# First panel of a two-block kernel by feature tiles, with squares on two engines, parameter rows issued around a square, and the 32-column panel in buffers of its own

## What is computed

```python
def _rms_norm(z, g):
    zf = z.astype(jnp.float32)
    zf = zf * lax.rsqrt(jnp.mean(zf * zf, axis=-1, keepdims=True) + RMS_EPS)
    return (zf * g.astype(jnp.float32)).astype(z.dtype)

def _token_mixer(xn, w_in, conv_a_w, shift_mu, w0, w2, a0, a2, g2, k_k, k_a, r_k, lnx_w, lnx_b, w_out):
    p = jnp.einsum('btd,de->bte', xn, w_in)
    gB, gC, hA = jnp.split(p[..., :3 * CONV_DIM], 3, axis=-1)
    ...
    q = p[..., 3 * CONV_DIM:]
    q = q + (_token_shift(q) - q) * shift_mu
    r, k, v, wd, ad, gd = jnp.split(q, splits, axis=-1)
    w_log = -jax.nn.softplus(-(w0 + jnp.tanh(wd) @ w2)) - 0.5
    decay = jnp.exp(-jnp.exp(w_log))
    a = jax.nn.sigmoid(a0 + ad @ a2)
    g = jax.nn.sigmoid(gd) @ g2
    kk = k4 * k_k;  kk = kk / jnp.maximum(jnp.linalg.norm(kk, axis=-1, keepdims=True), 1e-12)
    k4 = k4 * (1.0 + (a4 - 1.0) * k_a)
    ...
```

## Time and profile before

| | |
|---|---|
| median of 3 runs | 1960.25 us (1959.65 to 1961.53) |
| the profiled execution | 1962.35 us |
| its span in the trace | 1960.6 us |
| mean granted TensorE clock | 0.994 |
| PE busy | 1902.2 us, 12689 matmuls |
| DVE busy | 1154.5 us |
| ACT busy | 753.6 us |
| HBM read | 157.59 MB |

### The profile page before, as it was taken

How to read it: one execution, slowest core, us unless ns; L and a number is a source line. 1 busy time by engine, 2 the same in 40 slices (tenths; PEclk the granted TensorE clock), 3 DMA queues, 4 the chain that set the end, 5 groups by cost and what they waited for, 6 DMA issues and landing times.

```text
span 1960.6 us, 30342 instructions
## 1 busy us (share of the span) xinstructions
PE 1902.2 (97%) x12689; PEld 1536.9 (78%) x12689; DVE 1154.5 (59%) x1704; ACT 753.6 (38%) x1084; POOL 33.4 (2%) x72
## 2 busy tenths in 40 slices
PE   6989998999999999999999999999999999999999
PEld 4766777988888888787777778888778777778887
DVE  3574455677676336446687855455446678775544
ACT  4533423422222335533444334333533345334422
POOL 3000000020000000000000000000000000000000
PEclk9989999999999999999999999999999999999999
DMA  4221101433333232222222212233222212222232
GB/s 146 79 63 33 46 25 45 151 85 87 108 87 107 86 115 89 65 86 86 65 65 86 87 64 87 76 101 104 86 82 69 91 61 85 82 90 66 65 108 86
DMA packets 166036, 161.65 MB, mean 82 GB/s; under 512 B 13892, under 2 KB 150378, under 8 KB 165898
## 3 DMA queue, kind: packets, MB, share of 16 engines
q1 hardware_dynamic: 165200, 159.00, 25.9%
q10 hardware_dynamic: 698, 0.71, 0.1%
HBM read 157.59 MB, written 2.10 MB: 81 GB/s over the span
## 4 chain that ended last, share of the span: by engine, by line
PE 76%; DVE 2%; ACT 1%; issue 0%; ACTq 0%; DVEq 0%
PE psum L593 62%; PE psum L1911 5%; PE psum L2406 2%; PE psum L2383 1%; PE psum L583 1%; PE psum L2363 1%; PE psum L2391 1%; DVE w_lo L390 1%; PE psum L520 1%; ACT w_hi L349 1%; PE psum L529 0%; PE psum L2487 0%; DVE h_lo L454 0%; DVE ffn_normed L467 0%; PE psum L2472 0%; DVE w_lo L371 0%
## 5 line engine op out<-in xcount | busy, mean ns | idle before, releaser
L593 PE MATMUL psum<-h_hi,w_hi 128*128 128x512 f32 (+1 forms) x1592 | 622.4, 391 | 13.2 <-DVE h_lo L454 6.1
L593 PE MATMUL psum<-h_hi,w_lo 128*128 128x512 f32 (+1 forms) x1592 | 606.3, 381 | 0.0
L593 PE MATMUL psum<-h_lo,w_hi 128*128 128x512 f32 (+1 forms) x1592 | 606.2, 381 | 0.0
L390 DVE TENSOR_TENSOR w_lo<-w_raw,w_hi 128x2048 fp32r<-128x2048 f32 (+2 forms) x146 | 304.4, 2085 | 283.2 <-ACT w_hi L349 280.5
L349 ACT ACTIVATE w_hi<-w_raw 128x2048 fp32r<-128x2048 f32 (+1 forms) x151 | 265.0, 1755 | 370.9 <-PE psum L593 299.9
L593 PEld LDWEIGHTS psum<-h_hi,w_hi 128*128 128x128 f32 x1592 | 299.8, 188 | 92.8 <-issue 16.3
L593 PEld LDWEIGHTS psum<-h_hi,w_lo 128*128 128x128 f32 x1592 | 299.7, 188 | 58.4
L593 PEld LDWEIGHTS psum<-h_lo,w_hi 128*128 128x128 f32 x1592 | 300.1, 188 | 54.0 <-issue 0.2
L593 PE MATMUL psum<-w_hi,h_hi 128*128 128x512 f32 (+1 forms) x512 | 183.0, 357 | 2.7 <-DVE w_lo L390 1.8
L593 PE MATMUL psum<-w_lo,h_hi 128*128 128x512 f32 (+1 forms) x512 | 179.0, 350 | 0.0
L593 PE MATMUL psum<-w_hi,h_lo 128*128 128x512 f32 (+1 forms) x512 | 178.9, 349 | 0.0
(11 more groups left out here) (350 smaller groups left out, 2140.8 us busy)
## 6 DMA issues: line engine op xcount, KB each, us to landing
w_raw<-in_w_in_dram SPq DMA_DIRECT2D x170, 512.0 KB, 4.3
w_raw<-in_w_up_dram SPq DMA_DIRECT2D x44, 512.0 KB, 5.0
w_raw<-in_w_out_dram SPq DMA_DIRECT2D x24, 512.0 KB, 4.5
w_raw<-in_w_br_dram SPq DMA_DIRECT2D x48, 256.0 KB, 3.0
w_raw<-in_w_down_dram SPq DMA_DIRECT2D x22, 512.0 KB, 4.4
x_first<-in_x_dram SPq DMA_DIRECT2D x4, 512.0 KB, 4.9
x_tokens<-in_x_dram SPq DMA_DIRECT2D x4, 512.0 KB, 5.3
out_dram<-x_tokens SPq DMA_DIRECT2D x4, 512.0 KB, 2.6
```

Of the source, the lines that this page charges most:

```text
L390: eng.eng.tensor_tensor(m.wl[:, g % 2, 0:n], m.raw[:, g % 2, 0:n], m.wh[:, g % 2, 0:n].bitcast(F32), ALU.subtract).then_inc(eng.done, 1)
L593: last = pe.eng.matmul(out, a(k), b(k), start=(opens and k == 0 and i == 0), stop=(k == kt - 1 and i == 2), skip_group_check=ks is not None)
```

## The change

Buffers. Panel 0 now takes buffer 1 (`FIRST`), and the 32-column panel 1 has three small buffers of its own (`w1`, `w1H`, `w1L`, in the place of a decay tile that is written later). So panel 2 (buffer 0) is loaded and rounded without a wait, and panel 3 waits for panel 0.

ACT. A Sqrt of one constant stands first, and loads its table; POOL writes that constant before anything else. Six row loads, the square of x tile 0, the other six row loads, then the root of tiles 0 and 1 once DVE has squared tile 1 (a `tensor_tensor_reduce`), squares of tiles 2 and 3, their root, half of `w hi` 0, the eight `hH`, `w1 hi`, the row sums.

DVE. The square of tile 1; for each pair of tiles the reciprocal and the scaling, in halves of 512 columns (first halves of both tiles first), with the copy `params` between the pairs; the second half of `w hi` 0; the eight `hL` with the first half of `w lo` 0 behind the fourth and the second behind the eighth; `w1 lo`; the two `omm` steps.

PE. The sums table is turned without a wait for the rows. Feature tiles 0 to 3 are turned token tile by token tile, with the turn of the rows before token tile 2. Then for each feature tile k: two matmuls Whi·Hhi, two Whi·Hlo, and for k < 4 the turn of feature tile k + 4. Behind them panel 1's 16 with w1H, panel 0's 16 with wl, panel 1's 8 with w1L.

Later. PE runs half of panel 3 between the second and the third pair of `zw`, `za`. ACT and DVE split panel 2 in halves before shifted 0, panel 3 before shifted 2, panel 4 between the second and third pair (ACT) or behind k_scale 0 and 1 (DVE), and these two now stand before shifted 3 instead of behind decay_sum 1.

```diff
@@ lay_out
+    m.w1 = place("w_32_raw", [P, KT, 32], F32, m.Ep_at)
+    m.w1H = place("w_32_hi", [P, KT, 32], F32R, m.Ep_at + 4 * KT * 32)
+    m.w1L = place("w_32_lo", [P, KT, 32], F32R, m.Ep_at + 8 * KT * 32)
@@ constants
+    step(q.memset(m.eps[:, 0:1], RMS_EPS), "table 1")
+    step(q.memset(m.eps[:, 1:2], 1.0), "eps")
     step(q.memset(m.prow[:, :], 0.0), "prow zero")
...
@@ sync
+            if p == 1:
+                sp.dma_start(m.w1[:, :, :], s[:, :, c:c + w]).then_inc(w1_loaded, 16)
+                E.moved("w1 raw", "w1_loaded", 1)
+                continue
+            if p >= 3:
+                E.wait_ge(*E.point(("w lo", FIRST if p == 3 else p - 2)))
@@ tensor
-        turned("turn params", "params", [m.prow[:, :]])
-        turned("turn ind", ("ind", 1), [m.ind[:, i, :] for i in range(4)])
+        turn(E, m, banks, "turn ind", 3, ("ind", 1), [m.ind[:, i, :] for i in range(4)])
...
+        for t in range(TT):
+            if t == TT - 2:
+                E.wait_ge(*E.point("rows loaded"))
+                turn(E, m, banks, "turn params", 2, "params", [m.prow[:, :]])
+            E.wait_ge(*E.point(("n1", "xn a", t)))
+            for j in range(4):
+                last = pe.transpose(PS[:, 4 + j, P * t:P * t + P], m.xn1[:, t, P * j:P * j + P], m.ident[:, :])
...
+        E.wait_ge(act_done, E.at(("w hi half", FIRST)))
+        for k in range(KT):
+            E.wait_ge(act_done, E.at(("n1", "hi", k)))
+            if k == 4:
+                E.wait_ge(dve_done, E.at(("w hi", FIRST)))
+            for i in range(2):
+                pe.matmul(PS[:, i, :], H0[:, k, c0[i]], m.hH[:, k, :], start=k == 0, stop=False, skip_group_check=True)
+            E.wait_ge(dve_done, E.at(("n1", "lo", k)))
+            for i in range(2):
+                pe.matmul(PS[:, i, :], H0[:, k, c0[i]], m.hL[:, k, :], start=False, stop=False, skip_group_check=True)
+            if k < 4:
+                turn(E, m, banks, ("n1", "turn", k + 4), 4 + k, ("n1", "lo", k + 4),
+                     [m.xn1[:, t, P * (k + 4):P * (k + 4) + P] for t in range(TT)])
...
@@ tensor, zw and za
+            if j == 1:
+                panel(3, only=0)
-        panel(3)
+        panel(3, only=1)
@@ scalar
+        act.activation(m.stat[:, 5, 0:1], m.eps[:, 0:1], ACT.Sqrt).then_inc(act_done, 1)
...
+        rows_in(rowsrc[:6])
...
+        square(0)
+        rows_in(rowsrc[6:])
+        E.moved("rows loaded", "params_loaded", len(rowsrc))
+        E.wait_ge(dve_done, E.at(("n1", "ss", 1)))
+        root(0)
+        square(2)
+        square(3)
+        root(1)
...
@@ vector
+        dve.tensor_tensor_reduce(m.xn1[:, 1, :], m.x1[:, 1, :], m.x1[:, 1, :], 1.0, 0.0, ALU.mult, ALU.add,
+                                 m.stat[:, 0, 1:2]).then_inc(dve_done, 1)
...
+            for step, c in (("xn a", slice(0, D // 2)), ("xn", slice(D // 2, D))):
+                for t in (2 * g, 2 * g + 1):
+                    scaled(t, step, c)
+            if g == 0:
+                E.wait_ge(pe_done, E.at("turn params"))
+                dve.tensor_copy(m.pcol[:, :], PS[:, m.bank[E.key("turn params")], 0:P]).then_inc(dve_done, 1)
...
+        split(3)
+        shifted(2, then=False)
         E.wait_ge(act_done, E.at(("wsig", 0)))
         decay_sum(0)
+        k_scale(0)
+        k_scale(1)
+        split(4)
         shifted(3)
         E.wait_ge(act_done, E.at(("wsig", 1)))
         decay_sum(1)
-        k_scale(0)
-        k_scale(1)
```

More of the change, by code:

```diff
@@ new lines, in tensor @@
+        E.wait_ge(act_done, E.at("w1 hi"))
+        for k in range(KT):
+            for x in (m.hH, m.hL):
+                pe.matmul(PS[0:32, 2, :], H1[:, k, :], x[:, k, :], start=k == 0 and x is m.hH, stop=False,
+                          skip_group_check=True)
+        E.wait_ge(dve_done, E.at(("w lo", FIRST)))
+        for i in range(2):
+            for k in range(KT):
+                last = pe.matmul(PS[:, i, :], L0[:, k, c0[i]], m.hH[:, k, :], start=False, stop=k == KT - 1,
+                                 skip_group_check=True)
+            last.then_inc(pe_done, 1)
+            E.counted(("panel", 0, i))
@@ L736, in tensor @@
+        E.alias(("w used", FIRST), ("panel", 0, 1))
+        E.wait_ge(dve_done, E.at("w1 lo"))
+        for k in range(KT):
+            last = pe.matmul(PS[0:32, 2, :], L1[:, k, :], m.hH[:, k, :], start=False, stop=k == KT - 1,
+                             skip_group_check=True)
+        last.then_inc(pe_done, 1)
+        E.counted(("panel", 1, 0))
         E.wait_ge(*E.point("frows loaded"))
@@ L1103, in scalar, with rows_in, square @@
         E.wait_ge(act_done, E.so_far())
+        E.wait_ge(pool_done, E.at("eps"))
+        act.activation(m.stat[:, 5, 0:1], m.eps[:, 0:1], ACT.Sqrt).then_inc(act_done, 1)
+        E.counted(("n1", "table"))
         E.wait_ge(pool_done, E.at("prow zero"))
[L1105 to L1111, removed]
+        def rows_in(some):
+            for r0, src in some:
+                n, w = src.shape
+                act.dma_start(m.prow[r0:r0 + n, 0:w], src).then_inc(params_loaded, 16)
+        rows_in(rowsrc[:6])
+        def square(t):
+            E.wait_ge(act_done, E.so_far())
             E.wait_ge(*E.point(("x first", t)))
@@ L1134, in scalar @@
         E.wait_ge(act_done, E.so_far())
[L1135 to L1141, removed]
-        E.wait_ge(dve_done, E.at(("n1", "xn", TT - 1)))
+        E.wait_ge(dve_done, E.at(("n1", "xn", 3)))
         act.dma_start(m.w2a2[0:64, :], A["w2"][0]).then_inc(lr_loaded, 16)
@@ L1152, in scalar, with shifted @@
         z = 0
-        def shifted(p):
+        def shifted(p, then=True):
             nonlocal z
@@ L1166, in shifted @@
                 z += 1
-            split(p + 2)
+            if then:
+                split(p + 2)
         def decays(j):
@@ L1175, in decays @@
             E.counted(("Em", j))
-        shifted(0)
-        shifted(1)
+        split_hi_halves(E, m, 2, KT * panels[2][2])
+        shifted(0, then=False)
+        shifted(1, then=False)
         E.wait_ge(act_done, E.so_far())
@@ L1509, in prep @@
             E.counted(("prep", j))
-        shifted(0)
-        shifted(1)
+        split_lo_halves(E, m, 2, KT * panels[2][2])
+        shifted(0, then=False)
+        shifted(1, then=False)
         for b, n in ((0, FROWS), (1, FROWS2)):
```

133 lines of the change are left out of this document (85 added, 48 removed).

## The result

The changed kernel takes 1947.86 us (median of 4 runs, 1944.24 to 1949.99), against 1960.89 us for the kernel before (median of 4 runs beside them): a ratio of 0.9932, interval 0.9914 to 0.9949. The gain is 13.0 us where 16.3 were forecast; the median lies in the stated range (1939.5 to 1950.0), but outside the narrower forecast of 1940.7 to 1946.3. The profiled execution is the quickest of the four: 1944.24 us, span 1942.5, 18.1 us under the profiled execution of before. So what its trace shows has to be held against other executions before a term of the sum is judged by it.

A forecast was written before the change was run, and what follows sets the result against it. With TensorE busy 97% of the span, only its waits and low clock could yield gains. Gains of 8.8 + 6.3 + 1.2 = 16.3 us took the median of 1960.25 to 1944.0 us, range 1939.5 to 1950.0.

The forecast's parts named there:

- Rival A: Start gives less: rows up to 4 us late or clock low longer; gain 10 to 14, about 1948 us; chance 0.22.
- B: ACT replaces the bank wait between ffn rows and sum of squares; gain 4 to 10, about 1953 us; chance 0.09.
- D: hL or w_lo paces the first panel, PE reaches 43 as before; 0 to 4 us gained; chance 0.04.
- C: Wait before the spread shrinks by 2.6 us, or no clock fall there; 1938 to 1940.5 us; chance 0.08.
- Part 1: Start to the end of panels 0 and 1: ends at 34.9 instead of 43.69, gain 8.8 us, bounds 4 to 11.
- The first panel matmul: In the start: rows on PE at 11.5, first panel matmul at 14.7 against 25.52 before.
- The low rate: In the first panels: 3.5 us of low clock from 14.7 on, 1.8 us lost, bounds 0.7 and 5.1.
- The pacing: In the first panel: PE's 1.32 us per feature tile against DVE's 0.78, so PE, not h_lo, sets the pace.
- Rows and norm: In the start: rows land 4.9 us after last issue, at 11.5; squares and roots hidden, second table load gone.
- Part 2: Ffn rows to sum of squares: 38.0 becomes 31.7 us without bank wait or low clock; gain 6.3, bounds 2 and 6.5.
- Part 3: Wait of 6.58 us before the spread: two k scales earlier, gain 1.2 us (0 to 2.6).
- Everything after 115 us unchanged in length: From the chunk loop on: nothing changes in length, so what is gained by 115 us stays to the end.

The follow-up runs named there:

- The repeat: The changed kernel once more, nothing altered, for a second trace; 1950.85 us, ratio 0.9946 to the kernel before.
- rows first: The changed kernel with all twelve parameter row loads issued ahead of the square of x tile 0; 1945.03 us, ratio 0.9926.
- held clock: The changed kernel with 24 matmuls that nobody reads in the idle time before the spread of the norm rows; 1946.44 us, ratio 0.9926.
- start alone: The changed start and buffers, with the kernel before's order from panel 2 on; 1952.67 us, ratio 0.9960.
- panel 6 ahead: The changed kernel with the first half of panel 6 moved ahead of the spread of the norm rows; 1941.53 us, ratio 0.9906.
- the middle alone: The kernel before with only the later edits: half of panel 3 between the product pairs, splits of 3 and 4 and k scales moved; 1955.95 us.
- the busy start: The changed kernel with 13 transposes that nobody reads in PE's idle times between 7 and 14 us; 1947.20 us, ratio 0.9932.
- all three edits together: The changed kernel with 13 added start transposes, row loads ahead of the square, and half of panel 6 ahead of the spread; 1939.90 us.
- the kernel before with panel 6 ahead: The kernel before with only the first half of panel 6 moved ahead of the spread of the norm rows; 1954.72 us, ratio 0.9967.

## Why the prediction was right, and where its terms were off

The first median was in the range and the mechanism of the three parts as told; the sum was 3.3 us too good for the median of the first four runs, and 4.7 too good for all eight runs of the changed kernel taken together (median 1949.3 against 1960.9). The repeat's median, 1950.85, lies just above the range, so that the first one fell inside owes something to luck. Rival A, the start that gives less, is the nearest to what those eight show (1946 to 1950); of its conditions the longer low clock came, and the rows up to 4 us late did not. The others fell: no bank wait in part 2 (B), PE not paced at 43 (D), the wait not shrunk by 2.6 (C), and the kernel not slower: the longest low rate in its first panels was 6.3 us.

**Part 1, forecast 8.8.** The first trace gives 9.8 (43.69 - 33.85), the four others with this start unmodified up to the first panel 6.5 to 7.5 (ffn rows at 36.16, 36.64, 36.93, 37.16). The mark of the old start varies too (42.43 to 45.22 in four traces), so neither figure is good to better than about 1 us. Two terms were mis-sized, the chain from the rows to the first panel matmul and the low rate behind it.
The first panel matmul: 14.7 forecast, 14.9 to 15.8 measured. The rows came at 10.99 to 11.90, on both sides of 11.5; but from the rows to the first matmul it is 3.9 us, not 3.2. I counted one feature tile's transposes ahead of the first h_hi, and PE turns four of them, token tile by token tile: 8 transposes, 1.97 us from 12.63. And a scaling on DVE took 0.53 (2.12 for four), not 0.39. The forecast also has a slip of its own: 14.1 and an h_hi of 0.76 make 14.9, not 14.7.
The low rate: 1.3 us long in the first trace, 4.2 to 6.3 in the four others, where 3.5 was taken for the forecast. The stretch from the first panel matmul to the ffn rows (forecast 20.2) shows its price; the low rate is counted from the first panel matmul to where the matmuls begin to follow one another twice as fast:

| trace | low rate, us | stretch, us |
|---|---|---|
| changed, first | 1.3 | 18.9 |
| rows first | 2.0 | 19.2 |
| changed, second | 4.2 | 20.4 |
| held clock | 5.4 | 21.0 |
| start alone | 5.7 | 21.2 |
| panel 6 ahead | 6.3 | 21.4 |

Each stretch is 18.3 us and half of its low rate, to 0.1 us. So the price per microsecond was right, and the matmuls and turned tiles too (16.3 + 1.7 = 18.0); the length has no one size in executions of the same start. The loss by this is 0.65 to 3.2 us, where the bounds were 0.7 and 5.1. The 0.4 us that PE was to wait for the first h_lo did not come at the low rate; with the full rate from the start it was 0.6, and the stretch 19.2. The pacing was right: with the full rate a feature tile takes 1.36 us (16.53 to 17.89), forecast 1.32.

**Rows and norm.** The issue beside table load and square, the hidden square on DVE and the table load that is gone were right. That the landing goes by the last issue held in these traces: from it to the rows on PE it is 4.5 to 5.3 us in the ten traces in which PE waited for their landing, forecast 4.9, and no longer with the new start than with the old. That the square's wait holds the last six rows back was right too, but it costs less than its length: the last issue is at 6.28 to 7.40 with it (six traces) and at 6.36 and 5.81 without it.

**Part 2, forecast 6.3.** 6.0 in both traces of the changed kernel and 6.0 in the middle alone. What was saved by keeping ACT's bank wait off PE divides by the start-alone run: there the wait stays but no low clock follows, and 3.2 us are gained all the same. So by this one trace 3.2 us of the old 38.0 was the clock's, close to the 2.65 worked out from the earlier trace rows, and the interleaving of half a panel itself is worth the other 2.8 (the wait of 1.65, and 3.28 - 1.99 in the second group).

**Part 3, forecast 1.2.** 0.87. Two k scales moved (2.6 us of DVE), but the second shifted row waits for panel 4 on PE and starts at 72.72, and from there on the chain is what it was. The ACT row that shows it:

```profile
72.72 0.69 ACT L1239 ACTIVATE shifted<-psum,param_cols 128x512 f32<-128x512 f32 x1 [1.31 <-PE psum L597]
```

From the split behind it (w_lo at 75.52) on DVE is busy without a gap until 89.3, so only what lay ahead of 72.72 could be saved. From the second shifted row to the spread it is 23.9 us, before and after the change.

**The remainder.** This is the step that the forecast left out: nothing was to change after 115 us. With parts 1 to 3 at 7.0 (the middle of the five traces), 6.0 and 0.9 the sum is 13.9, and the eight runs gained 11.6. The second trace shows where such a difference sits: three low stretches after waits of 1.7 to 2.5 us between 309 and 388 us, 4.4 us in all. Over the changed kernel's eight executions the span is longer where the mean granted clock is lower: 1942.5 at 0.997, 1945.3 and 1945.7 at 0.996, 1947.0 at 0.995, 1948.3 to 1949.9 at 0.993; at the 0.51 granted in a low stretch, 0.001 of clock is an estimated 3.9 us of it, 1.95 us lost. The mean does not hold all of it, since the low rate of the first panel reads as 1.00 in it. "Everything after 115 us unchanged in length" was right for the instructions and their waits and wrong for the clock.

**Open.** Why these waits let the clock fall in some executions and not in others is not settled. The stretches appeared in the second trace of the changed kernel (3), the start alone (2), the busy start (2), all three edits together (3, one of them 6.8 us) and the kernel before with panel 6 ahead (1), beside the one near 750 us that all twelve traces have, and in none of the two traces of before, the first of after, the middle alone, panel 6 ahead, rows first or the held clock. The waits are the same in all of them (1.7 to 1.8, 1.9 and 2.5 us between 300 and 400 us). That is four of eight traces with the changed start and one of four with the old one, too few to say that the change makes them more frequent. The shifted start is not needed for it, as the kernel before with panel 6 ahead shows. No run was made that shifts the waits alone.
Nor is it settled what sets the length of the low rate at the start, which lasted 1.3 to 6.3 us in five executions of one order of work, or why the kernel before kept to a mean clock of 0.993 to 0.995 in every execution beside these runs.

## What to carry to other kernels

A wait of some microseconds on a busy TensorE can be worth more than its length: here 5.7 us of idle time cost 2.2 to 2.9 us more in the matmuls after it. First look for work of the next stage that is ready and can be cut in two; half a panel moved ahead of one wait brought 6.3 to 9.3 us in the changed kernel and 6.4 in the kernel before, over half of what the whole change brought, with two lines. And where a change moves the start, judge its terms from several traces: this one's quickest execution gave 9.8 us for a part that gave 6.5 to 7.5 in the four others.

## What the runs showed of the hardware

The granted clock read 1.00 while the first panel's matmuls ran at the low rate (in the changed kernel's second trace four transposes in 1.05 us instead of 0.60, a pair in 1.19 instead of 0.71), and so it did in the five other traces of this start without added transposes; there the rate has to be read from spacing.

With 13 transposes added between the real ones the first panel matmuls ran at the full rate in both traces (0.70 for a pair), and in none of the six traces of the same start without them (1.19 to 1.20).

In the ten traces in which PE waited for them, the rows were on PE 4.5 to 5.3 us after the last issue, whether that stood at 5.40 (kernel before) or at 7.40 (changed, second trace). Most single issues of a row load on ACT took 0.25 to 0.48 us, the first of each trace 0.58 or 0.59; eight between 4.5 and 5.5 us of the span took 0.59 to 0.99, which is not explained.

A low stretch of 3.4 us in the stream cost about 1.5 us (4.4 us for three, changed kernel, second trace against first); a wait that gives one in one execution gives none in the next (2.50 us of idle time at 379.08 in the first trace, none; at 385.16 in the second, 3.4 us).
